# Group norm held back by one prompt tile, and one tracker for each column block of actT

## What is computed

```python
o, R = retention(q, k, v, ret_state)          # 8 heads, DK 128, DV 256, chunks of 128 tokens
mu = jnp.mean(o, axis=-1, keepdims=True)
var = jnp.mean(jnp.square(o - mu), axis=-1, keepdims=True)
o = ((o - mu) * lax.rsqrt(var + EPS)).reshape(B, L, D_V) * gn_gain
r = jax.nn.silu(g_ret) * o
m = jax.nn.sigmoid(g_a) * a + jax.nn.sigmoid(g_r) * r
x1 = x + rmsnorm(m @ w_out, g_post_mix)
up = rmsnorm(x1, g_pre_ffn) @ w_up            # 2 * 5632 columns: values and gates
c = causal_dwconv(concat(conv_buf, up))       # 3 taps along the tokens
f = (gelu(c_gate) * c_val) @ w_down           # the product is actT below
y = x1 + rmsnorm(f, g_post_ffn)
```

## Time and profile before

| | us |
|---|---|
| median of 2 runs | 3824.04 |
| the two runs | 3716.74 and 3931.34 |
| the profiled execution, its time | 3701.64 |
| its span on the slowest core (core 0) | 3700.1 |
| spans of the eight cores | 3666.1 to 3700.1 |

### The profile page before, as it was taken

One profiled execution on the slowest core, in us unless ns is written; L12 is line 12 of the kernel. 1 busy time (PEld: TensorE's weight loads), 2 busy tenths in 40 slices (PEclk: granted clock), 3 DMA queues, 4 the chain that ended last, 5 costly groups with the idle time before them and its releaser, 6 DMA issues.

```text
span 3700.1 us, 37578 instructions; the slowest of 8 cores (3666.1 to 3700.1 us)
## 1 busy us (share of the span) xinstructions
PE 2543.7 (69%) x12512; PEld 1248.7 (34%) x12512; DVE 1469.2 (40%) x3224; ACT 706.6 (19%) x1120; POOL 326.9 (9%) x496
## 2 busy tenths in 40 slices
PE   5571943587746767676629399598973759777976
PEld 2231422233313322222214244353631324344543
DVE  4132546311224760465134412372734422255364
ACT  2122022221221110111011222321211121221110
POOL 0000011000000111111100000011110001000100
PEclk9885966799967888888859699798986879888988
DMA  9855495399994999999944046354544416544643
GB/s 199 209 140 143 144 271 187 53 193 211 224 201 88 187 200 205 184 188 188 233 150 162 29 163 228 107 195 165 198 154 171 137 59 204 205 136 141 213 143 121
DMA packets 264978, 622.16 MB, mean 168 GB/s; under 512 B 12954, under 2 KB 198682, under 8 KB 212548
## 3 DMA queue, kind: packets, MB, share of 16 engines
q0 software_dynamic: 212672, 416.00, 49.6%
q1 hardware_dynamic: 52116, 203.76, 15.0%
HBM read 593.17 MB, written 153.57 MB: 202 GB/s over the span
## 4 chain that ended last, share of the span: by engine, by line
PE 37%; DMA 30%; DVE 17%; issue 9%; ACT 7%; DVEq 1%; SPq 0%; ACTq 0%; POOL 0%; POOLq 0%
PE ps L563 23%; DMA arena<-w_up 10%; PE ps L1114 7%; DMA arena<-w_in 7%; DVE arena L1069 3%; DMA wsc<-arena 3%; DMA arena<-w_down 2%; PE ps L1037 2%; DVE arena L1066 2%; DVE arena L1072 2%; DMA arena<-w_pool 1%; ACT arena L538 1%; PE ps L546 1%; ACT arena L1098 1%; DMA arena<-sr 1%
## 5 line engine op out<-in xcount | busy, mean ns | idle before, releaser
L563 PE MATMUL ps<-arena 128*128 128x512 bf16 x4832 | 1081.3, 387 | 121.4 <-DMA arena<-w_in 53.7
L1037 PE MATMUL ps<-arena 128*128 128x384 bf16 (+1 forms) x4224 | 817.6, 358 | 121.7 <-DMA arena<-w_up 111.6
L563 PEld LDWEIGHTS ps<-arena 128*128 128x128 bf16 x4832 | 478.2, 100 | 720.6 <-issue 179.1
L1037 PEld LDWEIGHTS ps<-arena 128*128 128x128 bf16 x4224 | 422.5, 101 | 516.0 <-issue 204.9
L1114 PE MATMUL ps<-arena 128*128 128x512 bf16 x1584 | 377.2, 403 | 156.0 <-DVE arena L1101 105.3
L546 PE MATMUL ps<-arena 128*128 128x128 bf16 x432 | 50.3, 309 | 388.2 <-ACT arena L538 388.2
L134 POOL DMA_DIRECT2D arena<-wsc x280 | 149.2, 533 | 1885.5 <-PE ps L563 1046.6
L1114 PEld LDWEIGHTS ps<-arena 128*128 128x128 bf16 x1584 | 161.4, 103 | 371.4 <-issue 207.6
L1098 ACT ACTIVATE arena<-arena 128x384 f32<-128x384 f32 (+1 forms) x132 | 73.7, 558 | 659.0 <-DVE arena L1072 380.0
L546 PEld LDWEIGHTS ps<-arena 128*128 128x128 bf16 x432 | 43.9, 143 | 395.9 <-issue 395.9
L1061 DVE COPY arena<-arena 128x2 f32<-128x2 f32 x264 | 44.7, 169 | 333.2 <-ACT arena L1058 333.2
(11 more groups left out here) (130 smaller groups left out, 1850.0 us busy)
## 6 DMA issues: line engine op xcount, KB each, us to landing
arena<-wsc POOLq DMA_DIRECT2D x248, 1024.0 KB, 5.3
wsc<-arena SPq DMA_DIRECT2D x112, 1024.0 KB, 8.8
arena<-w_in POOLq DMA_DIRECT2D x44, 1024.0 KB, 26.7
arena<-w_up POOLq DMA_DIRECT2D x88, 512.0 KB, 8.2
arena<-xall SPq DMA_DIRECT2D x25, 1024.0 KB, 9.5
arena<-sr SPq DMA_DIRECT2D x32, 512.0 KB, 10.3
nr_s<-arena POOLq DMA_DIRECT2D x32, 512.0 KB, 8.0
arena<-w_down POOLq DMA_DIRECT2D x16, 1024.0 KB, 16.4
```

Source lines behind the costliest of these rows:

```text
L563: ins = e.matmul(PSf(bank), lhsT=hT[:, kc, tcol * 128:(tcol + 1) * 128], rhs=WB[wslot][:, kc, :], start=(kc == 0), stop=(kc == 15))
L1037: ins = e.matmul(ps[:, pb * 512:pb * 512 + N], lhsT=WB[wslot][:, kc, woff + jj * 128:woff + (jj + 1) * 128], rhs=hT[:, kc, 0:N], start=(kc ...
```

## The change

Three edits. (1) actT gets 22 trackers, one for each block jl, in place of one for the whole. A product on DVE writes its own; a down matmul group reads those of the 8 or 3 blocks that it multiplies. (2) The group norm is cut in two: o_evac copies the four banks of o to the tile's X buffer with ACT (4 instructions of 512 columns), and groupnorm_X takes the statistics and the normalization from that buffer, in place. (3) retention_prompt is cut in two, a (transposes and scores) and b (o, the state update, o_evac), and groupnorm_X of one prompt tile is recorded between a and b of the next; that of the last one comes at the end. The sample tile runs o_evac and groupnorm_X one after the other. The new trackers also join the list (PHB) from which the buffers that share their memory inherit their waits.

```diff
--- before.py
+++ after.py
@@ -327,6 +327,10 @@
         PHB = ["actT", "upv0", "upv1", "upg0", "upg1", "usv0", "usv1", "usg0", "usg1", "cv0", "cv1", "cg0", "cg1",
                "gl0", "gl1", "scT", "stg0", "stg1"]
 
+        actTT = [K.trk("actT%d" % j) for j in range(22)]
+        for j in range(22):
+            T["actT%d" % j] = actTT[j]
+        PHB += ["actT%d" % j for j in range(22)]
         S_X = [K.slot("X%d" % t, XT[t]) for t in range(4)]
         S_Y = [K.slot("Y%d" % t, [YT[t]]) for t in range(4)]
         S_WB = [[K.slot("WB%d_%d" % (i, h), [WBT[i][h]]) for h in range(2)] for i in range(2)]
@@ -645,10 +649,15 @@
             K.op("dve", lambda e: e.tensor_tensor(out=STm, in0=pv, in1=mb_, op=ALU.mult), reads=PST[6:8],
                  writes=[T["STm"]])
 
-        def groupnorm_to_X(t):
+        def o_evac(t):
+            for b in range(4):
+                K.op("act", lambda e, b=b: e.copy(out=Xf[t][:, b * 512:(b + 1) * 512], in_=PSf(b)),
+                     reads=[PST[b]], writes=XT[t])
+
+        def groupnorm_X(t):
             for h in range(8):
-                K.op("dve", lambda e, h=h: e.bn_stats(out=st6[:, h, :], in_=ps[:, h * 256:(h + 1) * 256]),
-                     reads=[PST[h // 2]], writes=[T["gnst"]])
+                K.op("dve", lambda e, h=h: e.bn_stats(out=st6[:, h, :], in_=Xf[t][:, h * 256:(h + 1) * 256]),
+                     reads=XT[t], writes=[T["gnst"]])
             for h in range(8):
                 K.op("dve", lambda e, h=h: e.bn_aggr(out=mv[:, h, :], in_=st6[:, h, :]), reads=[T["gnst"]],
                      writes=[T["gnst"]])
@@ -660,16 +669,21 @@
                  reads=[T["gnst"]], writes=[T["gnst"]])
             for h in range(8):
                 K.op("act", lambda e, h=h: e.activation(out=Xf[t][:, h * 256:(h + 1) * 256],
-                                                        in_=ps[:, h * 256:(h + 1) * 256], func=AF.Identity,
+                                                        in_=Xf[t][:, h * 256:(h + 1) * 256], func=AF.Identity,
                                                         scale=rs8[:, h:h + 1], bias=nm8[:, h:h + 1]),
-                     reads=[PST[h // 2], T["gnst"]], writes=XT[t])
+                     reads=XT[t] + [T["gnst"]], writes=XT[t])
             K.op("dve", lambda e: e.tensor_tensor(out=Xf[t], in0=Xf[t], in1=GB, op=ALU.mult),
                  reads=XT[t] + [T["GB"]], writes=XT[t])
 
-        def retention_prompt(t):
+        def groupnorm_to_X(t):
+            o_evac(t)
+            groupnorm_X(t)
+
+        def retention_prompt_a(t):
             qk_transposes(t)
             scores(t, 0)
 
+        def retention_prompt_b(t):
             def f(e):
                 for h in range(8):
                     o = ps[:, h * 256:(h + 1) * 256]
@@ -678,7 +692,7 @@
                 return ins
             K.op("pe", f, reads=[T["STm"], Xv[t], T["qkT"], T["Rbf"]], writes=PST[0:4])
             state_update_prompt(t)
-            groupnorm_to_X(t)
+            o_evac(t)
 
         def retention_sample(t):
             qk_transposes(t)
@@ -927,11 +941,18 @@
                             reads=[YT[i], T["sg%d" % j]], writes=[YT[i]])
                 if cb == 9:
                     load_gain(1)
+                    pend = None
                     for i, tl in enumerate(tiles):
                         if tl["kind"] == "sample":
                             retention_sample(i)
                         else:
-                            retention_prompt(i)
+                            retention_prompt_a(i)
+                            if pend is not None:
+                                groupnorm_X(pend)
+                            retention_prompt_b(i)
+                            pend = i
+                    if pend is not None:
+                        groupnorm_X(pend)
                     if tiles[-1].get("ret_out"):
                         K.dma("sp", nr_p.rearrange("h d v -> d h v"), Rf32, S_R, "store", is_output=True)
                     ck("p%d_ret" % pi)
@@ -1100,7 +1121,7 @@
                              reads=[T["cg%d" % rb]], writes=[T["gl%d" % rb]])
                         K.op("dve", lambda e, rb=rb, jl=jl: e.tensor_tensor(out=actT[:, jl, 0:N], in0=glb[rb][:, 0:N],
                                                                             in1=cvb[("v", rb)][:, 0:N], op=ALU.mult),
-                             reads=[T["gl%d" % rb], T["cv%d" % rb]], writes=[T["actT"]])
+                             reads=[T["gl%d" % rb], T["cv%d" % rb]], writes=[actTT[jl]])
                 ck("p%d_up%d" % (pi, hf))
                 out_tiles = [i for i, tl in enumerate(tiles) if tl.get("yout") is not None]
                 for nb in range(4):
@@ -1115,7 +1136,8 @@
                                                        rhs=WBd[wslot][:, kk, :], start=(q == 0 and kk == 0),
                                                        stop=(q == 1 and kk == 10))
                                     return ins
-                                K.op("pe", f, reads=[T["actT"], WBT[wslot][h]], writes=[PST[base + i]])
+                                K.op("pe", f, reads=actTT[q * 11 + DKH[h][0]:q * 11 + DKH[h][1]] + [WBT[wslot][h]],
+                                     writes=[PST[base + i]])
                             w_half_done(h)
                     for i in out_tiles:
                         if hf == 0:
```

## The result

| | before | after |
|---|---|---|
| median | 3849.45 us (10 runs) | 3655.54 us (11 runs) |
| lowest | 3695.61 us | 3632.43 us |
| profiled execution | 3701.64 us | 3642.1 us |
| spans of the cores | 3666.1 to 3700.1 us | 3603.7 to 3640.5 us |

The medians hold executions in which the cores of one die ran at a lower clock, more of them before than after, so they can't be set against each other; the ratio without those is **0.983**, interval 0.979 to 0.988: some 61 us off (3706.6 to 3645.4 as means), faster, not clearly by 2%.

A forecast was written before the change was run, and what follows sets the result against it. No engine bounds everything (PE 37%, DMA 30%, DVE 17% of the chain), so stages were priced singly: 49 + 10 + 19 = 78 us off 3701.6 gives 3624, forecast as 3625; 3605 to 3645 at 0.70, full range 3590 to 3745.

The forecast's parts named there:

- down in passes 1 and 2: Down matmuls start before the last product is made: 11.4 us saved in hf 0, 13 in hf 1, 49 over two passes.
- the retention: Group norm held back one tile: 4 us from six intervals, 18 at the ends, 3 lost on the sample tile; 19 together.
- T + 2.9: T is the end of a state update; after the last tile PE restarts 2.9 us later, before 8.8; 18 us in three passes.
- this is covered by about 7 us: After retention, ACT copies the next block's banks late, but PE has four other banks, so no loss, with 7 us spare.
- I take 5 for each, 10 us: Down in pass 0: the early start pays only DMA's idle time after each of two gaps; bounds 0 and 26 us.
- The sum: Whole kernel: 49 us from down in passes 1 and 2, 10 from pass 0, 19 from retention; 78 us off, ratio 0.979.
- the side of 2% that I gave the higher chance: Whole time: faster by over 2%, given 0.57, against 0.41 for within 2% and 0.02 for slower by over 2%.
- I forecast 3625, against executions like the profiled one: Whole time: 78 us taken off the profiled 3701.6, not the median shown, 3824; the same ratio there would give 3745.
- (a): Down: PE's early start is given back to weights in pass 0 and lower clock in passes 1, 2; 3662 us, chance 0.16.
- (b): Retention: the pipeline does overlap, statistics and aggregation vanish from six intervals, 45 us more; 3580 us, chance 0.03.
- (c): Retention: in-order DVE makes the held-back norm a new wait; slower, 3732 us if 12 us dearer per tile, chance 0.03.
- (d): Pass 0: both gaps before down are saved whole, 16 us more than forecast; 3608 us, chance 0.08.

## Why the prediction was right or wrong, point by point

**Right: down in passes 1 and 2.** Forecast 11.4 us for hf 0 and 13 for hf 1, 49 together. The rows show 37.0 - 26.0 = 11.0 and 36.8 - 23.1 = 13.7, the stage table 49 for the four. What was late next was what the prediction named: a bank in hf 0 (shown by moving the group), the last product in hf 1. The low clock came back behind the shorter waits as allowed for; the granted clock in the windows that hold them was 0.71 and 0.67:

```profile
2488.00:2493.00 5.00, 0.00 (x0) 0.00 (x0) 3.71 (x11) 1.27 (x3) 0.00 (x0) 0.71 0.26 80
2683.00:2688.00 5.00, 0.00 (x0) 0.00 (x0) 3.69 (x9) 0.52 (x1) 0.00 (x0) 0.67 0.59 210
```

**Right: the retention.** Forecast 27.6 us for an interval and 0.6 saved; measured 27.3. Forecast T + 2.9 for PE's restart; the last update ended at 2105.84, and PE started at 2108.51, T + 2.7. With the intervals this is 7 us in each of passes 1 and 2 (forecast 7.1) and 5.2 in pass 0 (4.1): 19 as forecast. That the pipeline hides almost nothing, because DVE runs the old norm ahead of the new update, was argued before and is now shown: with the update ahead of the wait for the normalization, the interval is 16 to 18 us.

**Right, with a term missing: "this is covered by about 7 us".** ACT's late copies delay nothing: PE waits for the last of them as long as before, 1.04 us. What the sum had at nothing is a lower granted clock behind the retention: blocks 0 and 1 and the pooling took 2.1 us more in pass 0 and the pooling 0.7 and 0.9 more in the others, 3.7 together.

**Mis-sized: "I take 5 for each, 10 us" in pass 0.** It measured 4 and 8 us in the two sets of profiles, about 6 over all, and DMA's idle time fell by 2.8 in hf 0 and 5.7 in hf 1. I read the idle time from two windows of one core and took it that no idle time would come up elsewhere; but loads also wait for the store from their half, and this holds them once the release no longer does.

**The sum.** With the terms as measured: 49 + 6 + 19 - 3.7 = 70 us. The means over all cores of the two pairs of profiles differ by 66.5 (3688.0 and 3621.5), the executions behind the ratio by 61 with an interval of 46 to 77 us. The forecast of 78 lies just outside. Of the 17 us between 78 and 61, 8 are the two terms above; the other 9 are not assigned, and scatter of the start of the program and of pass 0, 10 us and more from one execution to the next, is enough for them. Single executions in two later sets of runs, each on one chip, point the same way: 3715.7 against 3652.1 us in one (64 off), 3747.9 against 3683.8 and 3658.5 in the other (64 and 89). This makes 0.979 wrong for the side of 2% that I gave the higher chance.

**Wrong, and the step that failed: the base of the time.** "I forecast 3625, against executions like the profiled one". The median shown was 3824. Set against it, 3625 claims 199 us off, where the prediction's own sum has 78 and 61 were measured. The profiled execution was also a quick one: those behind the ratio have a mean of 3706.6, and the second profile of the same kernel took 3715.7, which makes up 5 of the 20 us between 3625 and 3645.4, the mean after. The sum belonged on the median shown, as a ratio, which gives 3745; the prediction has that figure only as an aside and as the end of its range. That the two medians of the result stand 194 us apart, close to the 199, is luck: nothing in the mechanism gives it. The mechanism, the waits and the overlap, held; in the sum itself the mis-sized terms are the two above, pass 0 with about 6 us for 10 and the clock behind the retention with 3.7 for nothing.

**The rivals.** (a), the start given back: not in passes 1 and 2, partly in pass 0. (b), full overlap: excluded by the 27.3 us, but reached by another order. (c), slower: the statistics from SBUF took 4.14 us, as from PSUM (4.17), the normalization 5.46 against 5.17; nothing near 9 us. (d), more from pass 0, 26 us: not seen, with 4 and 8. The edits to the fences cost nothing that a stage shows: the starts of passes 1 and 2 take 93 to 95 and 58 to 59 us in both kernels.

## What to carry to other kernels

Software pipelining on engines that run in order is decided by the order of the records, not by what is independent: before crediting an overlap, write down what stands ahead of the critical operation on its own engine, waits included. A tracker split finer than the last producer gains only as much work as there is before the first consumer of that last piece; the rest needs the producer itself to stop lagging, and here its lag was a short wait in each block (0.8 us of 5.7). A gain in a stage that DMA paces is bounded by the idle time of DMA over the whole stage and all cores, not by one window.

## What was unexpected

The statistics cost the same from SBUF as from PSUM: 0.427 us a piece (L659) against 0.430 (L650):

```profile
L671 ACT ACTIVATE arena<-arena 128x256 f32<-128x256 f32 x80 | 48.1, 601 | 13.5 <-DVE arena L667 7.0
L659 DVE BATCH_NORM_STATS2 arena<-arena 128x6 f32<-128x256 f32 x80 | 34.2, 427 | 29.2 <-ACT arena L654 22.0
```

The Trainium skill (Perfetto Trace Analysis, section Optimizing Scalar/DVE Operations) has 60 ns of access overhead for DVE on SBUF and 125 on PSUM; this operation doesn't show the difference. For ACT it has 93 and 51, and the trace agrees: 0.601 us from SBUF against 0.564 from PSUM.

A DVE wait of 0.8 us in each block of up was worth 39 us in passes 1 and 2 once the trackers were split.
